# Expert down product of a two-model forward pass: expert weights stationary, gated activations moving 256 wide

## The reference, cut to what matters

```
g   = softmax(top)
act = gelu(einsum('td,ted->te', x, u[eid]))
out = einsum('te,ted->td', g * act, v[eid])
```

## Time and profile before

| | us |
|---|---|
| median of 3 runs | 2824.53 |
| the runs | 2820.87, 2824.53, 2824.82 |
| the profiled execution | 2826.41 |
| its span, first to last instruction | 2824.2 |

### The profile page before, as it was taken

The page is one execution under the profiler, slowest core; times in us unless marked ns, Lnnn a source line. Parts: engine busy times, 40 slices in busy tenths (PEclk is TensorE's granted clock), DMA queues, the critical chain, the costliest instruction groups (busy, mean ns, idle before and its releaser), DMA issues.

```text
span 2824.2 us, 57248 instructions
## 1 busy us (share of the span) xinstructions
PE 2733.3 (97%) x19552; PEld 2562.9 (91%) x19552; DVE 2048.5 (73%) x4430; ACT 1453.7 (51%) x2378; POOL 178.8 (6%) x141
## 2 busy tenths in 40 slices
PE   7999999999999999989999999999999999999998
PEld 6999899999988888879999999988888889999998
DVE  8557997886567777876698888567777876666665
ACT  5455445444555555555544444455555565456544
POOL 0004000000000000000375000000000100000000
PEclk9999999999999999999999999999999999999999
DMA  5445566455766665424446555676666524563454
GB/s 191 169 161 181 193 218 215 175 180 191 244 247 241 241 241 190 143 87 165 165 164 220 189 181 173 215 253 241 241 241 241 189 91 166 193 223 123 179 193 179
DMA packets 140451, 546.19 MB, mean 193 GB/s; under 512 B 15784, under 2 KB 81592, under 8 KB 83616
## 3 DMA queue, kind: packets, MB, share of 16 engines
q1 hardware_dynamic: 63216, 455.38, 44.7%
q10 hardware_dynamic: 73728, 67.14, 7.5%
q0 software_dynamic: 3376, 21.88, 2.0%
HBM read 505.53 MB, written 40.91 MB: 193 GB/s over the span
## 4 chain that ended last, share of the span: by engine, by line
PE 72%; DVE 14%; DMA 4%; ACT 4%; issue 3%; POOL 2%; SPq 0%; ACTq 0%; DVEq 0%
PE bank L797 21%; PE bank L798 21%; PE bank L799 21%; DVE wL L552 5%; PE bank L1017 4%; DMA ring<-in_w_stream 4%; ACT wH L541 2%; POOL wL L552 2%; PE bank L918 1%; PE bank L938 1%; PE bank L929 1%; DVE pr_m L1974 0%; DVE ff_u L1771 0%; ACT ff_aH L1573 0%; DVE ff_f L2083 0%
## 5 line engine op out<-in xcount | busy, mean ns | idle before, releaser
L552 DVE TENSOR_TENSOR wL<-ring,wH 128x1024 fp32r<-128x1024 f32 x809 | 988.3, 1224 | 619.3 <-ACT wH L541 609.2
L541 ACT ACTIVATE wH<-ring 128x1024 fp32r<-128x1024 f32 x864 | 907.4, 1055 | 422.6 <-DMA ring<-in_w_stream 260.2
L797 PE MATMUL bank<-hnH,wH 128*128 128x256 f32 x3528 | 1007.8, 286 | 29.9 <-DVE wL L552 20.6
L798 PE MATMUL bank<-hnL,wH 128*128 128x256 f32 x3528 | 988.4, 280 | 0.0
L799 PE MATMUL bank<-hnH,wL 128*128 128x256 f32 x3528 | 985.9, 279 | 0.0
L797 PEld LDWEIGHTS bank<-hnH,wH 128*128 128x128 f32 x3528 | 666.0, 189 | 39.8 <-issue 19.9
L798 PEld LDWEIGHTS bank<-hnL,wH 128*128 128x128 f32 x3528 | 666.1, 189 | 0.6 <-issue 0.2
L799 PEld LDWEIGHTS bank<-hnH,wL 128*128 128x128 f32 x3528 | 665.4, 189 | 0.0
L797 PE MATMUL bank<-wH,wgtH 128*128 128x512 f32 x1024 | 398.5, 389 | 1.8 <-DVE wgtL L2011 1.8
L798 PE MATMUL bank<-wL,wgtH 128*128 128x512 f32 x1024 | 398.4, 389 | 0.0
L799 PE MATMUL bank<-wH,wgtL 128*128 128x512 f32 x1024 | 398.4, 389 | 0.0
(11 more groups left out here) (411 smaller groups left out, 3529.8 us busy)
## 6 DMA issues: line engine op xcount, KB each, us to landing
ring<-in_w_stream SPq DMA_DIRECT2D x432, 1024.0 KB, 4.9
act_parked<-act_out ACTq DMA_DIRECT2D x256, 128.0 KB, 3.0
act_in<-act_parked ACTq DMA_DIRECT2D x256, 128.0 KB, 2.7
sw_bias<-in_c_swa POOLq DMA_DIRECT2D x1, 4096.0 KB, 15.5
relb_rows<-rel_table POOLq DMA_DIRECT2D x1, 2048.0 KB, 9.8
h_parked<-h POOLq DMA_DIRECT2D x2, 1024.0 KB, 6.1
h_back<-h_parked POOLq DMA_DIRECT2D x2, 1024.0 KB, 7.6
od_relb<-relb_rows POOLq DMA_DIRECT2D x2, 1024.0 KB, 7.6
```

The costliest lines, as they stand in the source:

```text
L541: eng.activation(wH[:, b % NBUF, :], raw(b), ACT.Copy).then_inc(w_high, 1)
L552: eng.tensor_tensor(wL[:, b % NBUF, :], raw(b), wH[:, b % NBUF, :].bitcast(F32), ALU.subtract).then_inc(w_low, 1)
L797: pe.matmul(dst, lh, rh, start=start, stop=False, skip_group_check=True)
L798: pe.matmul(dst, lh, rl, start=False, stop=False, skip_group_check=True)
```

## The change

In the down product the 128x128 pieces of v become stationary, and the gated activations of all 256 tokens move. A block now takes eight pieces of 128 features, three matmuls of 256 columns each: 24 instead of 12. The sums have features on the partitions at once, so that copies, transposes and the tile `sums` go. Each bank of `psacc` holds two sums, one in each half; only the first matmul of a bank starts it. In the last block each of the eight sums is a group of its own (`sum` for `turned`) that counts in `group_done`; `v_done` then counts 127 blocks a layer, and the last block's weight buffer is freed by the last sum. The last four blocks are taken out of TensorE's loop. VectorE waits for both sums of a bank before it adds the first of them, and adds from the half of the bank. ScalarE waits for the last sum ahead of its sixth square, since `sq` overlies the gated rows. These rows are now taken from four elements behind the start of a longer tile, which makes the shared piece 8 elements longer; the relative bias moves into the arena, so that all tiles behind stay where they were.

```
-            blocks.append(((p + "v", n), ("peer", l, n)))
+            blocks.append(((p + "v", n), ("peer", l, n) if n < N_KEYS - 1 else (p + "sum", DC - 1)))
         for c in range(DC):
-            g((p + "turned", c), "dve")
+            g((p + "sum", c), "dve")
...
-        before.append(holder.get(turn))
+        before.append(None if key[0] in summed else holder.get(turn))
...
-        _, rel_bucket, rel_rows = stage(("rel_before", [MEM0 - 1024], F32), ("rel_bucket", [512], F32),
-                                        ("rel_rows", [512], F32))
+        _, rel_bias_sb, rel_bucket, rel_rows = stage(
+            ("rel_before", [MEM0 - 1032], F32), ("rel_bias_sb", [8], F32), ("rel_bucket", [512], F32),
+            ("rel_rows", [512], F32))
+        rb = rel_bias_sb[0:32]
...
-        act_in, wgtH, wgtL = stage(("act_in", [4, T], F32), ("wgtH", [2, T], F32R), ("wgtL", [2, T], F32R))
-        sb("shared", [P, DC * T])
-
-        rb = sb("rb", [32, 8])
+        act_in, wgt_rows = stage(("act_in", [4, T], F32), ("wgt_rows", [4 * T + 8], F32R))
+        wgtH, wgtL = [wgt_rows[:, 4 + 2 * T * i:4 + 2 * T * (i + 1)].rearrange("p (a b) -> p a b", a=2) for i in range(2)]
+        sb("shared", [P, DC * T + 8])
+
...
-                    for tt in range(NT):
-                        for half in range(2):
-                            last = product(psacc[2 * tt + half][:, :],
-                                           both(wgt, FULL, c % 2, slice(tt * P, (tt + 1) * P)),
-                                           both(blk, FULL, slice(half * 512, (half + 1) * 512)),
-                                           isinstance(i, int) and (i, c) == (0, 0), False)
-                    last.then_inc(v_done, 1)
+                    for d in range(DC):
+                        ending = isinstance(i, int) and (i, c) == (0, N_KEYS - 1)
+                        dst = bank((p + "sum", d)) if ending else psacc[d // 2]
+                        last = product(dst[:, d % 2 * T:(d % 2 + 1) * T], both(blk, FULL, slice(d * P, (d + 1) * P)),
+                                       both(wgt, FULL, c % 2), isinstance(i, int) and (i, c, d % 2) == (0, 0, 0), ending)
+                        if ending:
+                            last.then_inc(group_done, 1)
+                        elif d == DC - 1:
+                            last.then_inc(v_done, 1)
...
-                with pe.Fori(1, N_KEYS // 4) as i:
+                with pe.Fori(1, N_KEYS // 4 - 1) as i:
                     for j in range(4):
                         outs(i, j)
+                for c in range(N_KEYS - 4, N_KEYS):
+                    outs(0, c)
                 stands[0] = b0 + 2 * N_KEYS
-                for half in range(2):
-                    for by in (act_sums, dve_sums):
-                        pe.wait_ge(by, 2 * l + half + 1)
-                    for c in range(4 * half, 4 * half + 4):
-                        ps = bank((p + "turned", c))
-                        for tt in range(NT):
-                            last = pe.transpose(ps[:, tt * P:(tt + 1) * P], sums[:, tt, c * P:(c + 1) * P], ident)
-                        last.then_inc(group_done, 1)
...
+                    if name in ("mix1", "mix2") and c == 5:
+                        act.wait_ge(group_done, NO[(follows(name) + "sum", DC - 1)] + 1)
...
-                act.wait_ge(v_done, (l + 1) * N_KEYS)
-                for half in range(2):
-                    act.activation(sums[:, 0, half * 512:(half + 1) * 512], psacc[half][:, :],
-                                   ACT.Copy).then_inc(act_sums, 1)
...
-                dve.wait_ge(v_done, (l + 1) * N_KEYS)
-                for half in range(2):
-                    dve.tensor_copy(sums[:, 1, half * 512:(half + 1) * 512], psacc[2 + half][:, :]).then_inc(dve_sums, 1)
                 dve.wait_ge(h_back_in, 16 * (l + 1))
                 for c in range(DC):
-                    ps = take((p + "turned", c), False)
-                    dve.tensor_tensor(h[:, c, :], h_back[:, c, :], ps[:, 0:T], ALU.add).then_inc(read_by["dve"], 1)
+                    if c % 2 == 0:
+                        dve.wait_ge(group_done, NO[(p + "sum", c + 1)] + 1)
+                    ps = take((p + "sum", c), False)
+                    dve.tensor_tensor(h[:, c, :], h_back[:, c, :], ps[:, c % 2 * T:(c % 2 + 1) * T],
+                                      ALU.add).then_inc(read_by["dve"], 1)
```

More of the change, by code:

```diff
@@ L333, in build_stacks @@
     for n, (key, _) in enumerate(groups):
-        turned = ("peer0turned", "peer1turned")
-        turn = BANKS + key[1] if key[0] in ("peer0slotT", "peer1slotT") else key[1] if key[0] in turned else \
-            0 if groups[n - 1][0][0] in turned else turn
+        summed = ("peer0sum", "peer1sum")
+        turn = BANKS + key[1] if key[0] in ("peer0slotT", "peer1slotT") else BANKS + key[1] // 2 if key[0] in summed else \
+            0 if groups[n - 1][0][0] in summed else turn
         bank_of.append(turn)
-        before.append(holder.get(turn))
+        before.append(None if key[0] in summed else holder.get(turn))
         holder[turn] = n
@@ L358, in build_stacks @@
         (gates,) = stage(("gates", [N_KEYS, T], F32))
-        h_back, sums = stage(("h_back", [DC, T], F32), ("sums", [NT, D], F32))
+        (h_back,) = stage(("h_back", [DC, T], F32))
         MEM0, ATT0 = AR - 2 * DC * T - 56, AR - 2 * DC * T - 9344 - 8
@@ L489, in build_stacks @@
         act_back = [sem(f"act_back{i}") for i in range(4)]
-        act_sums, dve_sums = sem("act_sums"), sem("dve_sums")
         bucket_in, table_out, rows_out = [sem(n) for n in ("bucket_in", "rel_table_out", "relb_rows_out")]
@@ L533, in split_high @@
                 elif key[0] == "peer":
-                    eng.wait_ge(v_done, i * 4 + (key[1] * N_KEYS + key[2] + 1))
+                    eng.wait_ge(v_done, i * 4 + (key[1] * (N_KEYS - 1) + key[2] + 1))
                 elif key[0] == "rows":
@@ L622, in added @@
             if name in ("peer0", "peer1"):
-                read_of(eng, (name + "turned", c), eng is not act_engine)
+                read_of(eng, (name + "sum", c), eng is not act_engine)
             else:
@@ L673, in _ @@
             for dst, src in ((iww[:, :, :], iw_w), (snk[:, :], sinks),
-                             (rb[:, :], rel_bias)):
+                             (rb, rel_bias)):
                 pool.dma_start(dst, src).then_inc(cst_in, 16)
@@ L1104, in _ @@
             pe.wait_ge(bucket_in, 16)
-            pe.matmul(ps[0:8, :], rb[:, :], rel_bucket[0:32], start=True, stop=True).then_inc(group_done, 1)
+            pe.matmul(ps[0:8, :], rb, rel_bucket[0:32], start=True, stop=True).then_inc(group_done, 1)
             lin("even_in", range(3), hn, first=lambda k: normed("mix0", k))
@@ L1501, in weights_high @@
                     if not isinstance(i, int) or 4 * i + c >= 2:
-                        act.wait_ge(v_done, i * 4 + (l * N_KEYS + c - 1))
+                        act.wait_ge(v_done, i * 4 + (l * (N_KEYS - 1) + c - 1))
                     act.activation(wgtH[:, c % 2, :].unsqueeze(1), gates[:, bass.ds(i * 4 + c, 1), :],
```

## The result

The changed kernel takes 2835.79 us (median of 20 runs, 2824.29 to 2850.45), the one before 2824.68 (20 runs, 2817.57 to 2835.37): ratio 1.0045, 95% interval 1.0033 to 1.0057. It is 11.1 us slower; forecast was +7.7. Its times spread half as wide again, over 26 us instead of 18.

The account below looks back on a forecast made before the run. The prediction took TensorE's matmul pace to bound the kernel. Slower 256-wide matmuls (+11.3 us) and shorter layer ends (-3.6) summed to +7.7, 2832.2 us against the median; its own range was 2828 to 2836, the full range 2818 to 2845.

Parts of the forecast that it names:

- Layer 0: Layer 0's down product: no new stop, so it keeps the slow pace it is entered with, +10.4 us.
- Layer 1: Layer 1's down product: slow for eleven blocks, then the fast pace behind its stop, +0.9 us.
- The two draws that the prediction had: Feed-forward down products behind their first stops: the first ran at 113.3 ns, the second at 116.8.
- A demand slower by 0.9 us does not remove a stop of 1.77: Layer 1's down product: TensorE's stop, from ScalarE waiting for a weight block, remains despite the slower pace.
- The start address as the choice of rows: Down product: gated rows start four elements in, like the feed-forwards', so those stages' paces, 113.3 and 116.8 ns, are nearest.
- Layer's end: Down product's end: dropping copies, transposes and their waits saves 1.8 us a layer, both together -3.6, bounds -3.2 and -3.8.
- The new waits: Layer's end: ScalarE's wait ahead of its sixth square and VectorE's ahead of each second add cost nothing.
- That is where I see the extra 3 to 4 ns come from: 256-wide matmuls: the spare time a weight load had behind a 512-wide matmul is gone; stated without proof.
- Rival 2: Down product slow in both layers, weight load bounding each 256-wide matmul: +17.2 us, 2841.7; chance 24%.
- Rival 4: Down product: fixed cost for each matmul, the same everywhere, in place of two paces: +6.5 us, 2831.0; chance 4%.
- Rival 1: Down product at the fast pace in both layers: main part 0, leaving -3.6 us, 2820.9; chance 30%.

Follow-up runs that it names:

- run 1: The changed kernel again with no edit: 2850.98 us, ratio 1.0080.
- run 7: The changed kernel, with TensorE also waiting for the next block's gated rows ahead of every fourth down-product block, forcing stops: 2942.37 us.
- run 11: The changed kernel once more with no edit: 2842.92 us.
- run 12: The changed kernel a third time with no edit: 2851.67 us.
- all three repeats: The changed kernel with no edit, run 1, run 11 and run 12: 2850.98, 2842.92 and 2851.67 us.
- run 3: The changed kernel with its gated rows 0 instead of 4 elements into their tile (0 bytes instead of 16): 2868.34 us, ratio 1.0145.
- run 4: The changed kernel with its gated rows 8 instead of 4 elements into their tile (32 bytes instead of 16): 2841.99 us, ratio 1.0054.
- run 2: The kernel before, each 512-wide down-product matmul cut into two of 256, gated rows still stationary, old layer's end kept: 2864.86 us, ratio 1.0131.
- run 6: The changed kernel moving only 128 of 256 gated rows from each layer's second down-product block on, all weight loads kept: 3104.06 us.
- run 5: The changed kernel with high and low gated rows side by side, one 512-column matmul serving both, 16 loads a block: 2850.88 us, ratio 1.0073.
- run 9: Run 5's kernel (run 5), each block's eight wide matmuls first, then its eight narrow ones, rows 16 bytes into the tile: 2837.43 us, ratio 1.0043.
- run 10: As run 9, wide matmuls first, then narrow, but gated rows 0 bytes into the tile: 2846.89 us, ratio 1.0059.

## Why the prediction was right, and where not

**Layer 0: right.** "It should keep the slow pace it is entered with": +10.4 forecast, +10.32 measured, and 116.7 ns in all four profiles of the changed kernel. The 117.3 that it read from 45 matmuls ahead of the first feed-forward's stop is 116.7 by their starts; so short a count is coarse.

**Layer 1: the step that failed** is "behind it the pace is dealt anew; I take the fast one there: 11 x 0.081 = +0.9 us". That the pace is dealt anew held behind stops of 0.3 us and more (runs 1, 7, 11, 12). That the fast one comes did not: behind the stop came 118.7 in all three repeats, and behind run 7's forced stops 113.3 in 3 of 60. The two draws that the prediction had were from the feed-forwards, where the fast pace comes in 10 of 28; these odds did not carry over to the new tiles, though shape and offset are the same, and why is not known. Layer 1 cost +8.27 us in the profiled execution and 14.1 to 14.4 in the three repeats (364.17 to 364.47 us). "A demand slower by 0.9 us does not remove a stop of 1.77" failed as well: the stop shrank to 0.04 us in the profiled execution, too little to deal anew there, and to 0.3 to 0.6 in the repeats, each with 118.7 ns behind it. Without the 1.8 us that this gave back, the slow pace alone would have cost layer 1 some 10 us too.

**The start address as the choice of rows: right** (runs 3, 4). Rows 16 bytes in reach 113.3 ns now and then (run 7); those at 0 bytes did not in the one profile of run 3.

**Layer's end: mis-sized.** I took 1.8 us a layer with bounds of 1.6 and 1.9. Counted as there, from the last block's start, TensorE returned after 4.42 us instead of 6.56, 2.14 earlier. From the last start to the next it is 2.33, since the last matmul is narrower and the last block slower. Runs 2 and 3 isolate it, with the old and the new end at the same 120.0 ns: from last start to next start 3.95 and 1.67 us in layer 0. The square follows the last block's start by 2.94 us, not 3.1: ScalarE's two short activations start 0.11 us apart (1109.40, 1109.51), where I added two of 0.20.

**The new waits: right at nothing.** ScalarE's list of waits has none for the last sum: the last matmul starts at 1109.45, ahead of the first square, long before the sixth. What the squares wait for, up to 0.24 us each, are VectorE's adds.

**"That is where I see the extra 3 to 4 ns come from": half right.** Run 6 shows that pairs of load and matmul take 111.7 ns each though half the columns are gone, more than the 106.7 in which 256 columns pass at 2.4 GHz; so a narrow matmul has 1.6 ns to spare at 113.3. The Trainium skill, "TensorE: Matmul & The Clock Gate", section "LDWEIGHTS (loading the stationary operand)", gives a load P/1.2 ns for P columns, by estimate 106.7 ns for 128. Run 6's pace is 5 ns above that. But the load does not make the difference between 116.7 and 120.0: run 3 has the same loads and another start address for the moving rows. And with a third of the loads gone (runs 5, 9, 10) the time did not fall, since wide matmuls slowed down. How stream, load and address combine into these levels stays open.

**Rivals.** Rival 2's outcome, slow in both layers, is what all four profiles show; its price left out 118.7, and its reason, the load as the bound, gives 111.7 (run 6) and not 116.7. Rival 4's fixed cost fits at 0 bytes, with 13.3 ns a matmul over the columns at either width (run 2). The Trainium skill, "TensorE: Matmul & The Clock Gate", section "Back-to-back issue gap", has 2.5 for it, given for a single matmul and not for a stream of load and matmul pairs as here. Rival 1's pace never came in a whole layer of any profile.

**The time.** 2835.8 lies 3.6 above the forecast and well inside the range. It is not that near because the terms were that good: with layer 1 slow, the ends at -4.7 and the feed-forwards +5.5, the profiled execution came out at +19.5. The median of the 20 runs is lower than each of the four profiled executions (2842.92 to 2857.02), so many runs were faster somewhere. That they drew faster paces is likely but was not seen: the feed-forwards alone range from 60.85 to 67.36 us over the 14 profiles.

## What to carry to other kernels

Read a matmul's pace from starts in long stretches, in each stage apart; one good stretch of a shape is a draw, not its price, so look for every level the trace has and count how often each comes, in the stage itself: the same shape drew its fast pace in 10 of 28 cases in the feed-forwards and in 3 of 60 here. Halving the moving width takes away the cover of the weight load: ask what the loads alone would take (run 6 is the test: same loads, half the columns). Where the start address of a tile can be chosen, try several multiples of 16 bytes; here 16 bytes against 0 was worth 10 us a layer (358.29 against 368.52 in layer 0), nearly as much as the whole change cost.

## What the runs showed of the hardware

- One shape has four paces at one address (16 bytes off a multiple of 64): 113.3, 116.7, 118.7 and 120.0 ns. 116.7 and 118.7 held for thousands of matmuls without a change, 113.3 for the 461 behind a feed-forward's stop, and 120.0 came in a single stretch of 96 (run 7).
- 256-wide moving rows at a multiple of 64 bytes had only 120.0 ns in whole down products; 16 or 32 bytes further on, mostly 116.7 to 118.7.
- The granted clock fell to half, 1.2 of 2.4 GHz, behind a stop of 0.68 us in layer 1 of run 6 and stayed there though matmuls followed each other without a gap; behind a stop of 0.46 us in its layer 0 (785.59) the same row of matmuls kept 1.00. In run 5 a stop of 2.02 us (1905.38) was followed by a clock of 0.50 up to 1909.1, with 427 and 213 ns for the two widths, and then by 1.00 again.
- The length of a stop does not by itself tell whether the clock falls: behind all 60 stops of 1.3 us in run 7 and behind one of 2.63 us in run 12 it stayed at 1.00; behind 2.48 and 2.13 us in the changed kernel's feed-forwards it fell to 0.50 for 16 matmuls.
